# Five of the blocks that a two-layer trunk turns around: by 32x32 transposes of VectorE instead of TensorE and copies

## The chip, the cores and the metric

The kernel runs on one NeuronCore of a Trainium2 chip. The metric is the time of one execution on the device in microseconds (us), the median of several executions. The chip's engines are named as the profile names them: PE is TensorE (PEld its weight loads), DVE is VectorE, ACT is ScalarE, POOL is GpSimd, SP is SyncE, which here issues the weight transfers.

## What is computed

Two residual layers of a streaming encoder on 256 tokens of width 2048, in float32. The first layer's mixer has one input projection whose columns are q, k, v and g of a retention block and xb and gate of a gated recurrence (RG-LRU); the second layer's is windowed attention with grouped keys. Each layer ends in a squared-ReLU MLP. What matters here, cut from the reference:

```python
proj = h @ w_in                        # (256, 6144)
q, k, v, g, xb, gate = jnp.split(proj, cuts, axis=-1)
...
# RG-LRU: xc = causal 4-tap convolution of xb over time
r = sigmoid(einsum('bsnc,ncd->bsnd', xblk, w_a) + b_a)
i = sigmoid(einsum('bsnc,ncd->bsnd', xblk, w_x) + b_x)
log_a = -8 * r * softplus(-lam);  a = exp(log_a)
b = sqrt(-expm1(2 * log_a)) * i * xc
_, hh = lax.associative_scan(lru_combine, (a, b), axis=1)
lru_out = hh * gelu(gate, approximate=True)
...
q, k, v = jnp.split(h @ w_qkv, ...)    # attention: 4 key heads of 64
```

The recurrence runs along time, so xb and gate are wanted with channels on partitions and time along the free dimension; the projection gives them the other way round. The same holds for the keys of the attention.

## The kernel before

**Blocks and slots.** All dense products are cut into 89 blocks of 512 output columns (`BLOCKS`, L78): 12 of the first mixer's input projection in the order xb, gate, q, k, v, g (columns 0 to 511 of each), then the same six again, 4 of its output projection, 32 of the MLP, and so on; "kv" is the one block of keys and values of the second layer, "aq" its four query blocks. Each engine runs through the blocks in slots (`run_slots`, L182). In slot b TensorE multiplies block b in 8 halves (k = 0 to 7, 12 matmuls of 512 columns each, `products`, L1060), while ScalarE and VectorE finish block b-1 ("post", L649 and L943) at fixed halves (ticks) k of the slot, and prepare weights four halves ahead.

**Weights.** SyncE loads a block's weights in four transfers. For each half, ScalarE rounds 128x1024 values to `w_hi` (`cut_hi`, L540) and VectorE makes the rest `w_lo` (`cut_lo`, L737). At tick k of a slot both prepare half k+4, into a ring of four: `cut_hi` waits until TensorE is done with half k (`half_used`), `cut_lo` waits for `w_hi`, and TensorE's half k+4 waits for `w_lo` (`lo_ready`). Both calls stand last in a tick, behind what the tick does for the block before and for the recurrence.

**Turning a block.** ScalarE takes the finished block out of `acc` into `stage` (`leave`, L575, tick 0). For the plain kinds (xb, gate, q, k, kv, aq) TensorE then does 8 transposes of 128x128 into two PSUM banks (`turn_block`, L1097), at the end of half `TURN_AT` (2 for xb, gate and kv; 4 for q and k), and VectorE copies the two banks to the tile (L982) one tick later. The kinds "up" and "res" are turned by VectorE alone: 16 transposes of 32x256 (each four by two squares of 32x32) in `turn_quadrants` (L913), 4 at tick 1, 6 at tick 2 and 6 at tick 3 (`QUADRANTS_AT`, L98). In woven slots, of which kv's is one, everything comes two ticks later (`late`, L118).

**The recurrence.** For each of 8 channel groups n (`LRU_IN_SLOT`, L124: n = 0 in slot 2, 1 in slot 3, 4 in slot 8, 5 in slot 9) `lru` does, counted in ticks from its slot's start: convolution on VectorE at tick 2 (L820, L823); gate products on TensorE behind half 4 (L1136); sigmoids on ScalarE at tick 5 (L607) and there also the gelu's sigmoid (L610), which waits for GpSimd's polynomial of the gate (L526 to L528, `poly_done`); exp and tanh at tick 6 (L614, L616), a root at tick 7 (L620), the scan on VectorE at tick 8, that is tick 0 of the next slot (L836 to L845). GpSimd's polynomial for n = 0 and n = 4 waits for the gate block that has just been turned (`turned_out`). In slot 1, at tick 4, VectorE and ScalarE also make a small softplus table (L800 to L814; ScalarE's part is the exp of L699). In slots 3, 4, 9 and 10 VectorE rotates q or k at tick 1 (L788 to L793).

Slot by slot the blocks that the change touches are finished in slots 1 (xb, first half), 2 (gate, first half), 7 (xb, second), 8 (gate, second) and, in the second layer, that behind kv.

Of the kernel before, what the change touches and what calls it, by code (L numbers as in the profile page):

```python
# [30 lines left out]
QUADRANTS = P // QUAD  # L31
D_MODEL = 2048
SEQ = 256
TT = SEQ // P
KT = D_MODEL // P
NB = 512
# [53 lines left out]
TURNED = {"xb", "gate", "q", "k", "g", "kv", "aq", "up", "res"}  # L90
BY_QUADRANT = {"up", "res"}
SPLIT = {"g", "up", "res"}
PLAIN = TURNED - SPLIT
FROM_STAGE = {"xb", "gate", "kv", "aq"}

TURN_AT = {"aq": 0, "q": 4, "k": 4, "g": 4, "xb": 2, "gate": 2, "kv": 2}

QUADRANTS_AT = {"up": {1: 4, 2: 6, 3: 6}, "res": {1: 4, 2: 6, 3: 6}}  # L98
STATIONARY_STARTS = ({MIX_OUT0, MLP0, QKV0, ATT_OUT0, MLP1}
# [18 lines left out]
def late(b):  # L118


    return 2 if b in WOVEN else 0
# [26 lines left out]
N_EVAC_DVE = total({"res", "down", "fin"}, TT)  # L148
N_TURNED = total(TURNED, 2)
N_SPLIT = total(SPLIT, 2)  # L150

# [71 lines left out]
def build(nc, t):  # L223
    ctx = ExitStack()
    with ctx:
# [313 lines left out]
        def _(act):  # L539
# [35 lines left out]
            def leave(slot, kind, j):  # L575

                b = slot.b - 1
                act.wait_ge(half_used, slot.halves(late(b)))
                norm = NORM_OF[b]
                act.wait_ge(rinv_ready, norm + 1)  # L580
# [68 lines left out]
            def post(slot, k):  # L649
                b = slot.b - 1  # L650
                if b < 0:
                    return
                kind, j = BLOCKS[b]
                if k == late(b) and kind in BY_ACT:
                    leave(slot, kind, j)
                if k == 1 + late(b) and kind in ("res", "fin"):
                    act.wait_ge(evac_dve, slot.count(N_EVAC_DVE, 0))
                    square_sums(next_norm(b), j)
                if kind in SPLIT and k == out_at(kind, b):
                    hi, _, kt, scale = target(b)  # L660
                    for m in range(2):
                        turned_parts(hi, kt + 2 * m, None if scale is None else scale + 2 * m,
                                     slot.count(N_TURNED, -1, INIT_HALVES + m + 1), m, kind in BY_QUADRANT)
                if k == 4 and kind == "res" and j == COLS - 1:
                    root(next_norm(b))
# [62 lines left out]
        def _(dve):  # L728
# [184 lines left out]
            def turn_quadrants(slot, k, kind, j):  # L913
# [10 lines left out]
                if k == min(at) and kind == "res":  # L924
                    dve.wait_ge(evac_dve, slot.count(N_EVAC_DVE, 0))
                src = stage if kind == "up" else x[:, :, j * NB:(j + 1) * NB]
                src = src.rearrange("p t (k f c) -> p t k f c", k=COLS, f=QUADRANTS)
                dst = turn.rearrange("p m (k t a c) -> p t (m k) a c", k=2, t=TT, a=QUADRANTS)
                done = sum(n for tick, n in at.items() if tick < k)
# [4 lines left out]
                if k == max(at):  # L934
                    ins.then_inc(turned, 2)

            def plain_target(kind, j):
                if kind == "xb":
                    return lambda m: xb_t[:, 2 * m:2 * m + 2, TAPS - 1:]
                tile = {"gate": gate_t, "q": q_t, "k": k_t, "kv": kk_t, "aq": qq_t}[kind]  # L940
                return lambda m: tile[:, 2 * m:2 * m + 2, :]

            def post(slot, k):  # L943
# [30 lines left out]
                if kind in TURNED and k == out_at(kind, b):  # L974
                    for m in range(2):
# [4 lines left out]
                        elif kind in PLAIN:  # L980
                            dve.wait_ge(turned, slot.count(N_TURNED, -1, INIT_HALVES + m + 1))
                            nc.vector.tensor_copy(plain_target(kind, j)(m),  # L982
                                                  bank[:, m, :].rearrange("p (k s) -> p k s", k=2)
                                                  ).then_inc(turned_out, 1)
# [322 lines left out]
```

## Time and profile before

| what | value |
|---|---|
| median of 3 runs | 2023.03 us (2022.39 to 2023.51) |
| the profiled execution: its own time | 2022.12 us |
| its span, first to last instruction | 2020.2 us |
| PE busy | 2002.8 us (99%), 9195 matmuls |
| DVE busy | 1420.8 us (70%) |
| ACT busy | 1019.8 us (50%) |
| POOL busy | 45.2 us (2%) |
| mean granted clock of TensorE | 0.999 of full |

The share of PE is of modelled matmul ends, so "99% busy" says that it has hardly a gap, not that it is at its peak. The profile's other lists used below are: the waits (who waited for whom), the chain that ended last in order of time, and the timeline of each engine: start and length in us, the engine, the line, the operation, what is written and read, how many alike are merged into the row, and in brackets the idle time before it with what ended it.

### The profile page before, as it was taken

To read this page: it belongs to the slowest core of one execution; us is meant where nothing else is said; L and a number is where in the kernel's file an instruction comes from. 1 tells how busy PE (TensorE), PEld (TensorE's weight loads), DVE (VectorE), ACT (ScalarE), POOL (GpSimd) and SP (SyncE) were. 2 spreads that over 40 slices of the span, in tenths; PEclk is the share of its full clock that TensorE was granted. 3 is DMA by queue.
4 is the path that set the end of the run, shared out by engine and by line. 5 is a ranking of instruction groups with operands and counts; after the bars stand their busy time and mean duration, and the time that the engine had idled before them with its cause. 6 is when DMAs were issued, how large, how long until landed. Compare 5 with 4: busy or idle time off the path is not lost.

```text
span 2020.2 us, 24644 instructions
## 1 busy us (share of the span) xinstructions
PE 2002.8 (99%) x9195; PEld 1655.0 (82%) x9195; DVE 1420.8 (70%) x1932; ACT 1019.8 (50%) x1344; POOL 45.2 (2%) x55
## 2 busy tenths in 40 slices
PE   8999999999999999999999999999999999999998
PEld 6888888888888888888888877888888888888886
DVE  5776677988558657755889667988558756855875
ACT  6656665555345435434545555555435434444554
POOL 1110110000000000000000000000000000000000
PEclk9999999999999999999999999999999999999999
DMA  8556546656566565655655544566655665566563
GB/s 301 168 171 210 172 161 207 195 181 208 192 193 195 190 194 185 202 191 183 208 188 188 168 145 160 178 195 199 205 188 187 199 195 187 187 206 189 188 201 112
DMA packets 191100, 382.49 MB, mean 189 GB/s; under 512 B 6184, under 2 KB 6448, under 8 KB 190896
## 3 DMA queue, kind: packets, MB, share of 16 engines
q1 hardware_dynamic: 189776, 377.58, 57.4%
q0 software_dynamic: 1216, 3.88, 0.6%
q8 instruction: 49, 0.80, 0.2%
q14 instruction: 27, 0.22, 0.0%
q10 hardware_dynamic: 32, 0.01, 0.0%
HBM read 379.34 MB, written 2.10 MB: 189 GB/s over the span
## 4 chain that ended last, share of the span: by engine, by line
PE 95%; DVE 3%; ACT 2%; issue 0%; DMA 0%; SPq 0%; ACTq 0%
PE acc L1072 31%; PE acc L1074 30%; PE acc L1073 30%; ACT w_hi L550 1%; DVE w_lo L743 1%; PE bank L1103 1%; PE bank L1182 0%; DMA x<-in_x 0%; PE bank L1206 0%; PE bank L1192 0%; DVE area L823 0%; ACT L614 0%; ACT L620 0%; DVE turn L790 0%; PE bank L1136 0%
## 5 line engine op out<-in xcount | busy, mean ns | idle before, releaser
L743 DVE TENSOR_TENSOR w_lo<-raw,w_hi 128x1024 fp32r<-128x1024 f32 x712 | 865.3, 1224 | 538.4 <-ACT w_hi L550 535.9
L550 ACT ACTIVATE w_hi<-raw 128x1024 fp32r<-128x1024 f32 x712 | 748.1, 1059 | 811.2 <-PE acc L1074 810.2
L1072 PE MATMUL acc<-w_hi,a_hi 128*128 128x512 f32 x1568 | 615.1, 392 | 0.1
L1074 PE MATMUL acc<-w_hi,a_lo 128*128 128x512 f32 x1568 | 610.7, 389 | 0.0
L1073 PE MATMUL acc<-w_lo,a_hi 128*128 128x512 f32 x1568 | 610.5, 389 | 0.0
L1072 PE MATMUL acc<-w_hi,b_hi 128*128 128x512 f32 x1264 | 492.3, 390 | 0.0
L1073 PE MATMUL acc<-w_lo,b_hi 128*128 128x512 f32 x1264 | 491.8, 389 | 0.0
L1074 PE MATMUL acc<-w_hi,b_lo 128*128 128x512 f32 x1264 | 491.8, 389 | 0.0
L1072 PEld LDWEIGHTS acc<-w_hi,a_hi 128*128 128x128 f32 x1568 | 294.7, 188 | 62.9 <-issue 2.3
L1074 PEld LDWEIGHTS acc<-w_hi,a_lo 128*128 128x128 f32 x1568 | 294.4, 188 | 61.6
L1073 PEld LDWEIGHTS acc<-w_lo,a_hi 128*128 128x128 f32 x1568 | 294.6, 188 | 60.3
L1072 PEld LDWEIGHTS acc<-w_hi,b_hi 128*128 128x128 f32 x1264 | 237.2, 188 | 49.9 <-issue 0.7
L1074 PEld LDWEIGHTS acc<-w_hi,b_lo 128*128 128x128 f32 x1264 | 237.2, 188 | 49.2
L1073 PEld LDWEIGHTS acc<-w_lo,b_hi 128*128 128x128 f32 x1264 | 237.3, 188 | 49.2
L932 DVE STREAM_TRANSPOSE turn<-stage 32x256 f32<-32x256 f32 x512 | 223.1, 436 | 7.7
L558 ACT ACTIVATE b_hi<-turn 128x512 fp32r<-128x512 f32 x64 | 37.0, 625 | 107.1 <-DVE turn L932 107.1
L932 DVE STREAM_TRANSPOSE turn<-x 32x256 f32<-32x256 f32 x192 | 83.7, 436 | 2.9
L595 ACT ACTIVATE stage<-acc,rinv 128x512 f32<-128x512 f32 x92 | 57.6, 674 | 1.4 <-DVE rinv L776 1.4
L952 DVE TENSOR_TENSOR x<-x,acc 128x512 f32<-128x512 f32 x78 | 49.8, 679 | 0.0
L751 DVE TENSOR_TENSOR b_lo<-turn,b_hi 128x512 fp32r<-128x512 f32 x64 | 41.1, 684 | 0.0
L600 ACT ACTIVATE stage<-stage 128x512 f32<-128x512 f32 x64 | 36.7, 626 | 0.0
L560 ACT ACTIVATE a_hi<-turn,vecs 128x256 fp32r<-128x256 f32 x24 | 12.1, 502 | 35.8 <-DVE turn L932 35.8
(166 smaller groups left out, 566.6 us busy)
## 6 DMA issues: line engine op xcount, KB each, us to landing
raw<-in_mlp_w_up SPq DMA_DIRECT2D x128, 1024.0 KB, 5.5
raw<-in_mlp_w_down SPq DMA_DIRECT2D x128, 1024.0 KB, 5.1
raw<-in_hyb_w_in SPq DMA_DIRECT2D x48, 1024.0 KB, 5.2
raw<-in_attn_w_qkv SPq DMA_DIRECT2D x20, 1024.0 KB, 5.1
raw<-in_hyb_w_out SPq DMA_DIRECT2D x16, 1024.0 KB, 5.2
raw<-in_attn_w_out SPq DMA_DIRECT2D x16, 1024.0 KB, 5.2
x<-in_x SPq DMA_DIRECT2D x4, 512.0 KB, 9.7
out_y<-x SPq DMA_DIRECT2D x4, 512.0 KB, 3.0
```

The costliest lines, as they stand in the source:

```text
L550: nc.scalar.activation(w_hi[:, h % RING], raw[:, h // 2, 2 * (h % 2):2 * (h % 2) + 2, :], ACT.Copy).then_inc(hi_ready, 1)
L558: nc.scalar.activation(hi[:, kt:kt + 2, :], src, ACT.Copy).then_inc(turned_hi, 1)
L595: ins = nc.scalar.activation(stage[:, tt, :], src, ACT.Relu if kind == "up" else ACT.Copy, scale=s)
L600: nc.scalar.activation(stage[:, tt, :], stage[:, tt, :], ACT.Square).then_inc(squared, 1)
L743: nc.vector.tensor_tensor(w_lo[:, h % RING], raw[:, h // 2, 2 * (h % 2):2 * (h % 2) + 2, :], w_hi[:, h % RING].bitcast(F32), ALU.subtract) ...
L751: nc.vector.tensor_tensor(lo[:, kt:kt + 2, :], src, hi[:, kt:kt + 2, :].bitcast(F32), ALU.subtract).then_inc(turned_out, 1)
L932: ins = nc.vector.transpose(dst[f * QUAD:(f + 1) * QUAD, :, :, a, :], src[a * QUAD:(a + 1) * QUAD, :, :, f, :])
L952: nc.vector.tensor_tensor(xs, xs, acc[:, b % 2, tt, :], ALU.add).then_inc(evac_dve, 1)
L1072: nc.tensor.matmul(a, xh, wh, start=first, stop=False)
L1073: nc.tensor.matmul(a, xh, wl, start=False, stop=False)
L1074: ins = nc.tensor.matmul(a, xl, wh, start=False, stop=last)
L1103: ins = nc.tensor.transpose(bank[:, banks + m, e * SEQ + tt * P:e * SEQ + (tt + 1) * P], src[:, tt, c:c + P], ident[:, :])
```

## The change

For xb, gate and kv the 8 transposes on TensorE and the two copies on VectorE go. In their place `turn_quadrants` writes the final tile directly by 16 VectorE transposes at ticks 1, 2 and 3 (4, 6 and 6 of them). The last of the 16 gives the signal `turned_out`, which the copies gave. Since `stage` is read until then, `leave` of the block behind such a one waits for `turned_out` too. q, k and aq stay as they were.

```diff
+DIRECT = {"xb", "gate", "kv"}
+BY_QUADRANT = {"up", "res"} | DIRECT
-PLAIN = TURNED - SPLIT
-FROM_STAGE = {"xb", "gate", "kv", "aq"}
-TURN_AT = {"aq": 0, "q": 4, "k": 4, "g": 4, "xb": 2, "gate": 2, "kv": 2}
-QUADRANTS_AT = {"up": {1: 4, 2: 6, 3: 6}, "res": {1: 4, 2: 6, 3: 6}}
+PLAIN = TURNED - SPLIT - DIRECT
+FROM_STAGE = {"aq"}
+TURN_AT = {"aq": 0, "q": 4, "k": 4, "g": 4}
+QUADRANTS_AT = {kind: {1: 4, 2: 6, 3: 6} for kind in BY_QUADRANT}
...
                 act.wait_ge(half_used, slot.halves(late(b)))
+                if b > 0 and BLOCKS[b - 1][0] in DIRECT:
+                    act.wait_ge(turned_out, slot.count(N_TURNED, -1, INIT_HALVES))
...
+                if k == min(at) and kind in DIRECT:
+                    dve.wait_ge(evac_act, slot.count(N_EVAC_ACT, 0))
+                src = x[:, :, j * NB:(j + 1) * NB] if kind == "res" else stage
                 src = src.rearrange("p t (k f c) -> p t k f c", k=COLS, f=QUADRANTS)
-                dst = turn.rearrange("p m (k t a c) -> p t (m k) a c", k=2, t=TT, a=QUADRANTS)
+                if kind in DIRECT:
+                    tile = {"xb": xb_t[:, :, TAPS - 1:], "gate": gate_t, "kv": kk_t}[kind]
+                    dst = tile.rearrange("p k (t a c) -> p t k a c", t=TT, a=QUADRANTS)
+                else:
+                    dst = turn.rearrange("p m (k t a c) -> p t (m k) a c", k=2, t=TT, a=QUADRANTS)
...
                 if k == max(at):
-                    ins.then_inc(turned, 2)
+                    ins.then_inc(turned_out if kind in DIRECT else turned, 2)
```

What it moves on VectorE in slot 1, where the first xb block is finished (L743 and, in the changed kernel, L748 make `w_lo`; L800 and L805 begin the softplus). Before:

```order
L743 TENSOR_TENSOR w_lo<-raw,w_hi 128x1024 [waits hi_ready] x3
L982 COPY area<-bank 128x2x256 [waits turned] x2
L743 TENSOR_TENSOR w_lo<-raw,w_hi 128x1024 [waits hi_ready]
L800 TENSOR_SCALAR soft<-vecs 128x8 [waits vecs_ready,zeroed]
L801 TENSOR_TENSOR soft<-vecs,soft 128x8 [waits chain]
L803 TENSOR_SCALAR soft<-soft 128x8 [waits soft_exp]
```

and in the changed kernel:

```order
L748 TENSOR_TENSOR w_lo<-raw,w_hi 128x1024 [waits hi_ready]
L943 STREAM_TRANSPOSE area<-stage 32x2x4x32 [waits evac_act,turned_out]
L943 STREAM_TRANSPOSE area<-stage 32x2x4x32 x3
L748 TENSOR_TENSOR w_lo<-raw,w_hi 128x1024 [waits hi_ready]
L943 STREAM_TRANSPOSE area<-stage 32x2x4x32 x6
L748 TENSOR_TENSOR w_lo<-raw,w_hi 128x1024 [waits hi_ready]
L943 STREAM_TRANSPOSE area<-stage 32x2x4x32 x6
L748 TENSOR_TENSOR w_lo<-raw,w_hi 128x1024 [waits hi_ready]
L805 TENSOR_SCALAR soft<-vecs 128x8 [waits vecs_ready,zeroed]
L806 TENSOR_TENSOR soft<-vecs,soft 128x8 [waits chain]
L808 TENSOR_SCALAR soft<-soft 128x8 [waits soft_exp]
```

Two copies have gone and sixteen transposes stand among the four `w_lo` ahead of the softplus.

What it moves on VectorE in slot 2, where the first gate block is finished and the recurrence of n = 0 begins (the L820 and L823 rows, L825 and L828 in the changed kernel, are its convolution; "x6" and "x5" begin with the rest of slot 1). Before:

```order
L743 TENSOR_TENSOR w_lo<-raw,w_hi 128x1024 [waits hi_ready] x6
L820 TENSOR_SCALAR area<-area,vecs 128x256
L823 SCALAR_TENSOR_TENSOR area<-area,vecs 128x256 [waits chain] x3
L743 TENSOR_TENSOR w_lo<-raw,w_hi 128x1024 [waits hi_ready]
L982 COPY area<-bank 128x512 [waits turned] x2
L743 TENSOR_TENSOR w_lo<-raw,w_hi 128x1024 [waits hi_ready] x3
```

and in the changed kernel:

```order
L748 TENSOR_TENSOR w_lo<-raw,w_hi 128x1024 [waits hi_ready] x5
L943 STREAM_TRANSPOSE area<-stage 32x2x4x32 [waits evac_act,turned_out]
L943 STREAM_TRANSPOSE area<-stage 32x2x4x32 x3
L748 TENSOR_TENSOR w_lo<-raw,w_hi 128x1024 [waits hi_ready]
L943 STREAM_TRANSPOSE area<-stage 32x2x4x32 x6
L825 TENSOR_SCALAR area<-area,vecs 128x256
L828 SCALAR_TENSOR_TENSOR area<-area,vecs 128x256 [waits chain] x3
L748 TENSOR_TENSOR w_lo<-raw,w_hi 128x1024 [waits hi_ready]
L943 STREAM_TRANSPOSE area<-stage 32x2x4x32 x6
L748 TENSOR_TENSOR w_lo<-raw,w_hi 128x1024 [waits hi_ready] x3
```

Ten transposes now stand ahead of the convolution, and six behind it.

Who waits for the gate tile: ScalarE in slot 2, tick 4 to 6, the same rows in both kernels (here before; L610 is the gelu's sigmoid, which waits for GpSimd's polynomial):

```order
L550 ACTIVATE w_hi<-raw 128x1024 [waits half_used,raw_loaded0]
L607 ACT_TABLE_LOAD [waits soft_ready]
L607 ACTIVATE area<-bank,vecs 128x256 [waits gates_done]
L607 ACTIVATE area<-bank,vecs 128x256
L610 ACTIVATE area<-area 128x256 [waits poly_done]
L550 ACTIVATE w_hi<-raw 128x1024 [waits half_used]
L614 ACT_TABLE_LOAD
L614 ACTIVATE area<-area,soft 128x256 [waits sig_done]
```

Nothing moved here; the `w_hi` of the next halves and the rest of the recurrence stand behind the wait for `poly_done`.

## Rows read from the trace of the kernel before

**Rows 1.** The page, part 4: the chain that ended last, by engine.
```profile
PE 95%; DVE 3%; ACT 2%; issue 0%; DMA 0%; SPq 0%; ACTq 0%
```

**Rows 2.** The waits of the span: engine and line, releaser, us, times, longest.
```profile
PE bank L1136 <- DVE area L823: 1.2, 4, 0.3
```

**Rows 3.** The chain that ended last, in order of time: start us, us, what.
```profile
68.37 0.87 PE bank L1103 x8
```

**Rows 4.** Timeline of PE, slot 2: its first matmul, and the turn behind half 2.
```profile
60.05 0.39 PE L1072 MATMUL acc<-w_hi,a_hi 128*128 128x512 f32 x1
...
68.21 1.03 PE L1103 MATMUL bank<-ident,stage 128*128 128x128 f32 x8
```

**Rows 5.** The transposes of L932: count, duration ns min/median/max; then DVE's timeline.
```profile
L932 DVE STREAM_TRANSPOSE turn<-stage x512: 425/436/442, 425.7 to 1940.4; 32x256 f32<-32x256 f32 x171
...
401.20 2.67 DVE L932 STREAM_TRANSPOSE turn<-x 32x256 f32<-32x256 f32 x6
403.89 1.23 DVE L743 TENSOR_TENSOR w_lo<-raw,w_hi 128x1024 fp32r<-128x1024 f32 x1
```

**Rows 6.** Timeline of DVE, slot 1, from tick 0 to the weights behind the softplus.
```profile
43.88 2.36 DVE L743 TENSOR_TENSOR w_lo<-raw,w_hi 128x1024 fp32r<-128x1024 f32 x2 [2.34 <-ACT w_hi L550]
...
50.46 1.23 DVE L743 TENSOR_TENSOR w_lo<-raw,w_hi 128x1024 fp32r<-128x1024 f32 x1 [1.14 <-ACT w_hi L550]
...
56.59 3.49 DVE L743 TENSOR_TENSOR w_lo<-raw,w_hi 128x1024 fp32r<-128x1024 f32 x3
```

**Rows 7.** Timeline of ACT, slot 1: the softplus's exp begins.
```profile
52.04 1.28 ACT L699 ACT_TABLE_LOAD   x1 [1.62 <-DVE soft L801]
```

**Rows 8.** Timeline of DVE, slot 2: weights, convolution, weights, copies.
```profile
64.12 1.23 DVE L743 TENSOR_TENSOR w_lo<-raw,w_hi 128x1024 fp32r<-128x1024 f32 x1 [1.55 <-ACT w_hi L550]
...
67.92 0.41 DVE L820 TENSOR_SCALAR area<-area,vecs 128x256 f32<-128x256 f32 x1
...
69.81 1.22 DVE L743 TENSOR_TENSOR w_lo<-raw,w_hi 128x1024 fp32r<-128x1024 f32 x1
70.94 1.28 DVE L982 COPY area<-bank 128x512 f32<-128x512 f32 x2
```

**Rows 9.** Timeline of POOL: first and last operation of the polynomial, n = 0, then n = 1.
```profile
72.31 0.61 POOL L526 TENSOR_TENSOR area<-area 128x256 f32<-128x256 f32 x1 [50.60 <-DVE area L982]
...
73.50 1.59 POOL L528 TENSOR_TENSOR area<-area 128x256 f32<-128x256 f32 x1
...
89.23 1.46 POOL L526 TENSOR_TENSOR area<-area 128x256 f32<-128x256 f32 x1 [10.08 <-DVE area L845]
...
91.58 1.05 POOL L528 TENSOR_TENSOR area<-area 128x256 f32<-128x256 f32 x1
```

**Rows 10.** Timeline of ACT, slot 2: the gelu's sigmoid, and the weights behind it.
```profile
77.91 0.42 ACT L610 ACTIVATE area<-area 128x256 f32<-128x256 f32 x1
78.35 1.06 ACT L550 ACTIVATE w_hi<-raw 128x1024 fp32r<-128x1024 f32 x1
```

**Rows 11.** Timeline of DVE from slot 2's last tick on; and of PE, slot 3, gate products.
```profile
85.29 1.23 DVE L743 TENSOR_TENSOR w_lo<-raw,w_hi 128x1024 fp32r<-128x1024 f32 x1 [1.45 <-ACT w_hi L550]
...
98.53 0.70 PE L1136 MATMUL bank<-area 128*128 128x256 f32 x2 [0.30 <-DVE area L823]
```

**Rows 12.** Slot 8: DVE's weights at tick 0, and ACT's weights behind its L610.
```profile
209.26 1.23 DVE L743 TENSOR_TENSOR w_lo<-raw,w_hi 128x1024 fp32r<-128x1024 f32 x1 [1.55 <-ACT w_hi L550]
...
223.52 1.06 ACT L550 ACTIVATE w_hi<-raw 128x1024 fp32r<-128x1024 f32 x1 [1.45 <-PE acc L1074]
```

**Rows 13.** Timeline of DVE: slot 7, weights at tick 0; and the slot behind kv, tick 3.
```profile
186.61 1.23 DVE L743 TENSOR_TENSOR w_lo<-raw,w_hi 128x1024 fp32r<-128x1024 f32 x1 [1.55 <-ACT w_hi L550]
...
1122.70 0.29 DVE L971 COPY area<-area 64x256 f32<-64x256 f32 x1
```

**Rows 14.** PE's second turn of x after an idle stretch; and that stretch in windows (the 1.00 is the granted clock).
```profile
10.46 1.97 PE L1103 MATMUL bank<-ident,x 128*128 128x128 f32 x8 [2.39 <-DMA x<-in_x]
...
10.40:12.00 1.60, 1.54 (x7) 1.54 (x8) 1.60 (x4) 1.60 (x3) 0.00 (x0) 1.00 1.04 367
```

More of the change, by code:

```diff
@@ L90 @@
 TURNED = {"xb", "gate", "q", "k", "g", "kv", "aq", "up", "res"}
-BY_QUADRANT = {"up", "res"}
+DIRECT = {"xb", "gate", "kv"}
+BY_QUADRANT = {"up", "res"} | DIRECT
 SPLIT = {"g", "up", "res"}
-PLAIN = TURNED - SPLIT
-FROM_STAGE = {"xb", "gate", "kv", "aq"}
-TURN_AT = {"aq": 0, "q": 4, "k": 4, "g": 4, "xb": 2, "gate": 2, "kv": 2}
-QUADRANTS_AT = {"up": {1: 4, 2: 6, 3: 6}, "res": {1: 4, 2: 6, 3: 6}}
+PLAIN = TURNED - SPLIT - DIRECT
+FROM_STAGE = {"aq"}
+TURN_AT = {"aq": 0, "q": 4, "k": 4, "g": 4}
+QUADRANTS_AT = {kind: {1: 4, 2: 6, 3: 6} for kind in BY_QUADRANT}
 STATIONARY_STARTS = ({MIX_OUT0, MLP0, QKV0, ATT_OUT0, MLP1}
@@ L149 @@
 N_TURNED = total(TURNED, 2)
+N_MOVED = total(TURNED - DIRECT, 2)
 N_SPLIT = total(SPLIT, 2)
@@ L662, in post @@
                         turned_parts(hi, kt + 2 * m, None if scale is None else scale + 2 * m,
-                                     slot.count(N_TURNED, -1, INIT_HALVES + m + 1), m, kind in BY_QUADRANT)
+                                     slot.count(N_MOVED, -1, INIT_HALVES + m + 1), m, kind in BY_QUADRANT)
                 if k == 4 and kind == "res" and j == COLS - 1:
@@ L925, in turn_quadrants @@
                     dve.wait_ge(evac_dve, slot.count(N_EVAC_DVE, 0))
-                src = stage if kind == "up" else x[:, :, j * NB:(j + 1) * NB]
+                if k == min(at) and kind in DIRECT:
+                    dve.wait_ge(evac_act, slot.count(N_EVAC_ACT, 0))
+                src = x[:, :, j * NB:(j + 1) * NB] if kind == "res" else stage
                 src = src.rearrange("p t (k f c) -> p t k f c", k=COLS, f=QUADRANTS)
-                dst = turn.rearrange("p m (k t a c) -> p t (m k) a c", k=2, t=TT, a=QUADRANTS)
+                if kind in DIRECT:
[3 more added lines that the diff above has]
+                    dst = turn.rearrange("p m (k t a c) -> p t (m k) a c", k=2, t=TT, a=QUADRANTS)
                 done = sum(n for tick, n in at.items() if tick < k)
@@ L934, in turn_quadrants @@
                 if k == max(at):
-                    ins.then_inc(turned, 2)
+                    ins.then_inc(turned_out if kind in DIRECT else turned, 2)
             def plain_target(kind, j):
-                if kind == "xb":
-                    return lambda m: xb_t[:, 2 * m:2 * m + 2, TAPS - 1:]
-                tile = {"gate": gate_t, "q": q_t, "k": k_t, "kv": kk_t, "aq": qq_t}[kind]
+                tile = {"q": q_t, "k": k_t, "aq": qq_t}[kind]
                 return lambda m: tile[:, 2 * m:2 * m + 2, :]
@@ L980, in post @@
                         elif kind in PLAIN:
-                            dve.wait_ge(turned, slot.count(N_TURNED, -1, INIT_HALVES + m + 1))
+                            dve.wait_ge(turned, slot.count(N_MOVED, -1, INIT_HALVES + m + 1))
                             nc.vector.tensor_copy(plain_target(kind, j)(m),
```

## Prediction

> **What bounds the kernel now.** I read the chain that ended last first. It lies on PE for 95% [rows 1], so TensorE's stream of matmuls is the time, and what another engine does counts only where TensorE has to wait for it. The list of waits comes second. Behind the start, nearly the only such wait that it books to another engine is the gate product of the recurrence waiting for the convolution on VectorE: 1.2 us in four waits, the longest 0.3 [rows 2]. They stand in slots 3, 4, 9 and 10, in which VectorE rotates q or k. So these four slots have no cover left at all. Third come the timelines of VectorE, ScalarE and GpSimd in the slots that the change touches, which show how far each is ahead of TensorE there.
>
> **What goes.** A turn on TensorE adds 0.87 us to the chain [rows 3], five times: 4.35 us at most. The copies are worth 1.28 us of VectorE per block [rows 8], but only where VectorE is waited for.
>
> **What comes.** 16 transposes per block. The same form runs 704 times before at 425 to 442 ns [rows 5]; six in a row and the step to the next operation take 2.69 us (401.20 to 403.89), so four take 1.79, and a `w_lo` with the step to a transpose 1.25. A block costs VectorE 7.17 us where the copies cost 1.28. I go through the five slots and ask each time when the last work behind the transposes is ready and when it is wanted. A half on TensorE takes (68.21 - 60.05) / 3 = 2.72 us [rows 4].
>
> **Slot 1 (xb, first half).** VectorE's tick 0 starts with `w_lo` at 43.88, not changed, since that time comes from ScalarE [rows 6]. From there it never idles: 1.25 + 1.79 (four transposes) + 1.25 + 2.69 + 1.25 + 2.69 puts the `w_lo` of tick 3 at 54.80, against 50.46 before, 4.34 us later. The exp of the softplus on ScalarE starts 1.58 behind that `w_lo` (50.46 to 52.04) [rows 7], so at 56.38, and the next `w_lo` 4.55 behind the exp's start (52.04 to 56.59), so at 60.93; it ends at 62.16. That `w_lo` is of tick 4: half 0 of slot 2. TensorE, rid of one turn, wants it at 60.05 - 0.87 = 59.18 [rows 4]. So it waits 3.0 us and slot 2 starts at about 62.2 instead of 60.05. Term: **+2.2 us**. The rest of slot 1 is in time: half 7 is wanted at 62.2 - 3.0 - 2.7 = 56.5 and its `w_lo` (tick 3) ends at 56.0. Weights for halves 1 to 3 of slot 2 then follow at VectorE's pace, 1.13 us apiece, ahead of TensorE's 2.72.
>
> **Slot 2 (gate, first half).** I keep the clock of before, since all engines start this slot off TensorE. VectorE: `w_lo` at 64.12 [rows 8], then 1.25 + 1.79 + 1.25 + 2.69 = 71.10 when the ten first transposes are done. The convolution takes 1.89 (67.92 to 69.81), to 72.99. TensorE wants it behind half 4, at 68.21 + 2 x 2.72 = 73.65: just in time. Then 1.25 + 2.69: the gate tile is complete at 76.93 (before: 72.22, the end of the copies). GpSimd starts its polynomial 0.09 us behind that (72.22 to 72.31), at 77.02. The polynomial took 2.78 us for n = 0 (72.31 to 75.09), where VectorE was idle for its first part, and 3.40 for n = 1 (89.23 to 92.63) beside VectorE's work [rows 9]. VectorE now has two `w_lo` to do just there, and none behind them; I take 3.2: ready at 80.2. ScalarE's L610, which waits for it, starts at 80.25 instead of 77.91 [rows 10]: **2.35 us later**. Queued behind L610 on ScalarE are the weights `w_hi` of ticks 5, 6 and 7 and between them two table loads, exp, tanh and root, back to back in the trace; VectorE's `w_lo` of tick 7 (85.29) waits for the last of them, and from there VectorE runs without a gap (scan, `w_lo`, rotation, `w_lo`, convolution of n = 1) to TensorE's gate products at 98.53, for which TensorE already waits 0.30 [rows 11]. So the whole 2.35 arrives at TensorE in slot 3, and the turn saved in slot 2 only makes the wait longer. Term: **+2.35**. In slots 3 and 4 all then counts from TensorE again.
>
> A rule of the Trainium skill bears on this term: the page "GPSIMD Engine Reference", section "Specifications", says that GpSimd's access is shared with VectorE and contended while VectorE runs an instruction with two SBUF inputs (`w_lo` is one). The trace agrees: the same first operation took 0.61 us with VectorE idle and 1.46 beside it [rows 9]. Without such contention the polynomial would be at its 2.78 or under, and the term 1.9.
>
> **Slot 8 (gate, second half).** The same 12.81 us from the `w_lo` of tick 0 (64.12 to 76.93): 209.26 + 12.81 = 222.07 [rows 12], GpSimd 0.09 + 3.2, and 0.05 and 0.44 to the `w_hi` behind L610 (77.91 to 78.35 [rows 10]): 225.85, against 223.52. There ScalarE had 1.45 us of idle time, which is used up in this. The chain behind it is that of slot 3. Term: **+2.35** (225.85 - 223.52, rounded).
>
> **Slot 7 (xb, second half)** has no softplus and no recurrence. From 186.61 [rows 13] the `w_lo` of tick 3 is done 12.2 us later, at 198.8; TensorE wants it for half 7 at about 201.6, the turn already taken off. Cover: 2.8 us. Term: **-0.87**. **The slot behind kv**: transposes begin at 1122.99 [rows 13] and VectorE is through with them at 1132.6, level with TensorE again by the next block; the tightest `w_lo` (tick 5) ends at 1133.8 and is wanted at 1135.5. Term: **-0.87**.
>
> **The new waits.** `leave` behind a direct block waits for transposes that ended four ticks earlier: nothing.
>
> **Sum**: 2.2 + 2.35 + 2.35 - 0.87 - 0.87 = +5.2 us, on the profiled execution's own 2022.12 (its span 2020.2 and 1.9 around it). The median is 0.91 above that execution, so I add to the median: **2028.2 us**. Bounds: transposes at 425 or 442 ns move each of three terms by -0.2 or +0.1; the polynomial at 2.78 us, or half a microsecond above 3.2, moves two terms by -0.45 or +0.5; TensorE's restart in slot 2 may cost 0.2 more. That gives +3.7 to +6.7, or 2026.7 to 2029.7.
>
> **The rivals.**
> **Faster: VectorE's delay stays covered everywhere.** Then only the five turns count: -4.35, 2018.7 us. It decides where the delays shrink below their cover: in slot 1 the transposes would have to take 3.0 us less, 0.25 us apiece instead of 0.44. For it speaks that "up" and "res" blocks are turned this way without a wait on PE in the list; against it that neither has a softplus or a polynomial behind the transposes, and 704 durations that agree within 4%. The Trainium skill (page "VectorE: DVE Perf Modes", section "The three transpose paths") gives 311 ns for a 128x128 on VectorE, in bf16; a block of eight would be an estimated 2.5 us by that, and this rival would hold. The trace disagrees for float32 in this form, 7.0 us for sixteen. The same page's rules advise TensorE for a 128x128 transpose whose result may go to PSUM, which is what the kernel does before. Chance 0.08.
> **In between: L610 costs nothing.** If ScalarE's delay is caught up before slots 3 and 9 (a cover that I overlook between 78 and 98 us), those terms are 0 at best instead of 2.35, and the sum is +2.2 - 1.74 = +0.5: 2023.5. The trace speaks against it, with the waits of 0.3 at the very end of that chain [rows 2, 11]. The same result, give or take a microsecond, if the softplus is covered and L610 is not (4.7 - 3 x 0.87 = +2.1: 2025.1). Chance 0.17.
> **Dearer: TensorE restarts slowly.** It now stands for 3.0 us once and for some 2.5 us twice. After such a stretch at the start (2.39 us) eight transposes took 1.97 us instead of 1.03, at a granted clock that the windows show as 1.00 (2.4 GHz) [rows 14, 4]. Three times 0.94 more is 2031.0. The page "TensorE: Matmul & The Clock Gate" (section "The HAM clock gate") holds that an idle array is put to half its clock until it has been busy again; the row shows half speed, the windows no lower clock, so it is open. Chance 0.08.
> That the change does not do what it says I leave out: the order of instructions shows the transposes, and no turn on TensorE, in all five slots.
>
> **How the numbers follow.** The forecast's own case has 0.67. A measurement of this kernel tells about 0.2% (4 us) from no change, so slower begins at 2027.1, a microsecond below the forecast: 0.61 of the 0.67 and the dearer case, 0.69 in all. Faster begins at 2019.0: 0.07. The rest, 0.24, is within. The range holds the forecast's bounds and half of the two neighbours: 2024.5 to 2030.8.
>
> **What would show it.** Waits of PE on `w_lo` of about 3 us at the start of slot 2 (near 60 us) and on the convolution or the rotation in slots 3 and 9, 3 us or more each, with ScalarE's L610 (its new line) waiting for GpSimd for 2 to 3 us twice; transposes into `area` at 436 ns; no PE wait in slots 7 and behind kv, each 0.87 shorter. Wrong would be: no wait before slot 2 (the softplus had cover), L610 without a wait, or transposes into the tiles that cost something else than those into `turn`.

## The result, and the profile after

The changed kernel takes **2036.86 us** (median of 6 runs, 2035.6 to 2038.05), the kernel before in the same session 2022.71 us (2022.36 to 2023.51). The ratio is 1.0068, with a 95% interval of 1.0058 to 1.0078: slower by 14 us. The forecast was 2028.2 us, and 2030.8 the end of its range: the direction was right and the size too small by a factor of nearly three. The profiled execution took 2035.6 us, its span is 2033.8 (13.6 more than before).

The page of the changed kernel (TensorE's lines are 9 higher than before; L550, L610, L699, L743, L823 and L932 are now L552, L615, L704, L748, L828 and L943): one queue of part 3, the chain that ended last by engine (part 4), and one group of part 5.

```profile
q8 instruction: 66, 1.08, 0.2%
...
PE 92%; DVE 4%; ACT 2%; issue 1%; POOL 0%; DMA 0%; ACTq 0%; SPq 0%; DVEq 0%
...
L943 DVE STREAM_TRANSPOSE area<-stage 32x256 f32<-32x256 f32 x80 | 34.8, 436 | 1.2
```

PE has 92% of the chain and not 95 [rows 1]. The 80 transposes take 436 ns each, as reckoned. The first line has changed: the engines' code came in 66 packets, before in 49 (0.80 MB). I come back to it. The waits (who for whom: us in all, times, longest):

```profile
ACT area L615 <- POOL area L530: 8.7, 2, 5.1
...
ACT L704 <- DVE soft L806: 6.9, 1, 6.9
...
PE bank L1145 <- DVE area L828: 5.1, 4, 2.3
...
PE acc L1081 <- ACT stage L600: 3.0, 1, 3.0
PE bank L1112 <- DVE turn L798: 2.9, 2, 1.4
...
PE acc L1081 <- issue: 0.9, 2, 0.5
```

Of PE's four, before had only the first, with 1.2 us [rows 2]; the other three are new. ScalarE's wait on the softplus (second row) was 1.6 us before, its wait on GpSimd not there. I followed each to its place.

**Slot 1 to 2.** Timeline of the changed kernel, rows of DVE, ACT and PE in order of time:

```profile
55.07 1.23 DVE L748 TENSOR_TENSOR w_lo<-raw,w_hi 128x1024 fp32r<-128x1024 f32 x1
...
56.66 1.28 ACT L704 ACT_TABLE_LOAD   x1 [6.85 <-DVE soft L806]
...
59.20 0.39 PE L1083 MATMUL acc<-w_hi,a_lo 128*128 128x512 f32 x1
...
61.22 4.62 DVE L748 TENSOR_TENSOR w_lo<-raw,w_hi 128x1024 fp32r<-128x1024 f32 x4
...
62.58 0.77 PE L1081 MATMUL acc<-w_hi,a_hi 128*128 128x512 f32 x1 [2.99 <-ACT stage L600]
63.15 0.63 PE L1082 MATMUL acc<-w_lo,a_hi 128*128 128x512 f32 x1
63.57 0.63 PE L1083 MATMUL acc<-w_hi,a_lo 128*128 128x512 f32 x1
```

This execution is 0.33 us late from slot 1 on. Without that, the three times on VectorE and ScalarE were forecast within 0.1 (54.80, 56.38, 60.93), and slot 2's first matmul comes 2.20 late. (The list names ScalarE's copy of the finished block, which ended just then, at 62.5. It is not what TensorE waits for: before, the same copy starts at 61.21, after slot 2's first matmul at 60.05 [rows 4]. The `w_lo` of 61.22 to 62.45 is.) But then the matmuls start 0.43 us apart instead of 0.23. The windows of the changed kernel show why (us, busy and count of PE, PEld, DVE, ACT, POOL, then the granted clock):

```profile
62.00:65.00 3.00, 2.42 (x6) 1.99 (x7) 3.00 (x4) 1.10 (x2) 0.00 (x0) 0.51 0.17 20
106.00:110.00 4.00, 4.00 (x12) 3.14 (x11) 3.81 (x5) 1.15 (x3) 1.55 (x1) 0.57 0.77 247
254.00:260.00 6.00, 6.00 (x15) 4.67 (x16) 4.38 (x5) 1.14 (x3) 0.74 (x1) 0.50 0.86 297
```

TensorE ran at half clock (1.2 GHz) in three stretches, each behind one of the new waits; before, all three windows show 1.00 with 15, 20 and 28 matmuls in them.

**Slot 2 to 3.** The same timeline: POOL's polynomial, ACT behind it, and PE in slot 3:

```profile
80.92 1.65 POOL L528 TENSOR_TENSOR area<-area 128x256 f32<-128x256 f32 x1 [59.32 <-DVE area L943]
82.67 1.25 POOL L529 TENSOR_SCALAR area<-area 128x256 f32<-128x256 f32 x1
84.00 0.74 POOL L530 TENSOR_TENSOR area<-area 128x256 f32<-128x256 f32 x1
...
84.77 0.42 ACT L615 ACTIVATE area<-area 128x256 f32<-128x256 f32 x1 [3.64 <-POOL area L530]
...
101.91 1.09 PE L1112 MATMUL bank<-ident,turn 128*128 128x128 f32 x8 [1.45 <-DVE turn L798]
105.26 0.70 PE L1145 MATMUL bank<-area 128*128 128x256 f32 x2 [2.26 <-DVE area L828]
```

The polynomial took 3.82 us (80.92 to 84.74), not the 3.2 I had taken. The chain behind it is the one forecast, and it reaches TensorE twice in slot 3, at the turn of q and at the gate products. Slots 8 and 9 repeat it.

**The first MLP loop.** Timeline of PE where the loop over 8 slots of the first MLP, which runs three times, jumps back:

```profile
601.64 0.39 PE L1083 MATMUL acc<-w_hi,a_lo 128*128 128x512 f32 x1
602.39 0.49 PE L1081 MATMUL acc<-w_hi,a_hi 128*128 128x512 f32 x1 [0.36 <-issue]
...
776.36 0.39 PE L1083 MATMUL acc<-w_hi,a_lo 128*128 128x512 f32 x1
777.27 0.49 PE L1081 MATMUL acc<-w_hi,a_hi 128*128 128x512 f32 x1 [0.52 <-issue]
```

Two gaps that no engine and no transfer of data explains, in code that the change does not touch. The list of DMA queues for 590 to 900 us, which is the second and third pass, has this row in the changed kernel:

```profile
q8 instruction: 17, 0.28, 0.4%
```

In the kernel before it has no row for that queue: no code came while the loop ran again. The 17 packets are all that the changed kernel has more than before (66 against 49).

**The ledger.** Time of like events after less before, from both timelines; each line is what it grew by:

| place | forecast | measured |
|---|---|---|
| start, up to slot 1 | 0 | +0.33 |
| slot 1 to 2, wait on the softplus's chain | +2.2 | +2.20 |
| half clock behind it | 0 | +1.45 |
| slot 2 to 3, chain of the gelu's sigmoid | +2.35 | +2.75 |
| half clock behind it | 0 | +1.62 |
| slot 7, turn of xb gone | -0.87 | -0.92 |
| slot 8 to 9, the same chain | +2.35 | +2.69 |
| half clock behind it | 0 | +2.93 |
| jumps back of the first MLP loop | 0 | +0.65, +0.82 |
| kv, turn gone | -0.87 | -0.93 |
| sum | +5.2 | +13.6 |

Against the forecast that is 8.4 us more: 6.0 are the clock, 1.5 the loop, 0.7 the chain with the polynomial, 0.3 the start. My theory from here on: *the forecast's waits are right; the clock falls because of them; and the loop's gaps come from where its code lies.* The rivals: the clock falls for another reason (VectorE's load, DMA), and the loop's gaps belong to the direct transposes.

### The profile page after: what moved, and what is told of

Same layout as the page of the kernel before. It is cut to its first block, busy times and chain, and to the rows that moved or that the text cites. A ratio compares the mean times of both kernels' runs of the same rounds, so it can differ in the third digit from the quotient of the medians.

```text
span 2033.8 us, 24622 instructions
## 1 busy us (share of the span) xinstructions
PE 2005.5 (99%) x9155; PEld 1655.2 (81%) x9155; DVE 1449.9 (71%) x2002; ACT 1018.8 (50%) x1344; POOL 46.8 (2%) x55
## 4 chain that ended last, share of the span: by engine, by line
PE 92%; DVE 4%; ACT 2%; issue 1%; POOL 0%; DMA 0%; ACTq 0%; SPq 0%; DVEq 0%
PE acc L1081 30%; PE acc L1083 30%; PE acc L1082 30%; ACT w_hi L552 1%; DVE w_lo L748 1%; DVE area L943 1%; DVE area L828 0%; PE bank L1191 0%; PE bank L1215 0%; PE bank L1201 0%; PE bank L1112 0%; ACT L619 0%; ACT L625 0%; DMA x<-in_x 0%; DVE turn L795 0%
## 5 line engine op out<-in xcount | busy, mean ns | idle before, releaser
L748 DVE TENSOR_TENSOR w_lo<-raw,w_hi 128x1024 fp32r<-128x1024 f32 x712 | 865.7, 1226 | 521.3 <-ACT w_hi L552 518.4
L552 ACT ACTIVATE w_hi<-raw 128x1024 fp32r<-128x1024 f32 x712 | 747.2, 1059 | 803.0 <-PE acc L1083 802.1
L943 DVE STREAM_TRANSPOSE turn<-stage 32x256 f32<-32x256 f32 x512 | 223.0, 436 | 7.7
L943 DVE STREAM_TRANSPOSE turn<-x 32x256 f32<-32x256 f32 x192 | 83.6, 436 | 2.9
L943 DVE STREAM_TRANSPOSE area<-stage 32x256 f32<-32x256 f32 x80 | 34.8, 436 | 1.2
```

What stands on the lines that cost most here:

```text
L552: nc.scalar.activation(w_hi[:, h % RING], raw[:, h // 2, 2 * (h % 2):2 * (h % 2) + 2, :], ACT.Copy).then_inc(hi_ready, 1)
L748: nc.vector.tensor_tensor(w_lo[:, h % RING], raw[:, h // 2, 2 * (h % 2):2 * (h % 2) + 2, :], w_hi[:, h % RING].bitcast(F32), ALU.subtract) ...
L943: ins = nc.vector.transpose(dst[f * QUAD:(f + 1) * QUAD, :, :, a, :], src[a * QUAD:(a + 1) * QUAD, :, :, f, :])
```

## The experiments

Twelve kernels. In most only some of the five blocks are direct; the code for that is the change's own with a set of pairs:

```diff
-DIRECT = {"xb", "gate", "kv"}
+DIRECT = {("xb", 0)}          # or the pairs named in each experiment
```

**1 to 3: parts of the change.** xb's first half alone:

> Only the first xb block is turned by VectorE, the other four as before. Theory A (the cost is where TensorE waits, plus half clock after a long wait): one wait of 3.0 us ahead of slot 2, slot 2 starts 2.2 us later than before, its first seven matmuls at half clock add 1.4; in all +3.6 us against before, about 2026.3, with one stretch of granted clock 0.50. Theory B (every directly turned block costs alike, a fifth of the 13.6 us of the whole change): +2.7, and no such wait stands out. If the stall without the clock were all: +2.2.

Measured: 2034.54 us (2033.44 to 2036.87), ratio 1.0061 [1.0046, 1.0077]. Both gate blocks alone:

> Only the two gate blocks are turned by VectorE. Theory A: no wait ahead of slot 2; ScalarE's gelu sigmoid waits 3.6 to 5 us for GpSimd's polynomial in slots 2 and 8, TensorE reaches the gate products of n=1 and n=5 2.7 us late each, and after each wait runs at half clock for 3.4 to 6.9 us, 1.6 to 2.9 us more: +8.6 to +11.2 against before, about 2032.6. Theory B (a fifth per block): +5.4. Without the clock: +5.4 as well, but then no stretch of granted clock under 1.00 is to be seen.

Measured: 2034.82 us (2034.22 to 2035.45), ratio 1.0059 [1.0044, 1.0075]. xb's second half and kv alone, the two that I had called covered:

> Only the second xb block and kv are turned by VectorE. Theory A: both have cover, so only two turns go: -1.8 us, about 2020.9, no new wait of TensorE. Theory B (a fifth per block): +5.4. If the matmuls that are gone shift the code of TensorE's first MLP loop so that its instructions are fetched again in every pass, +1.5 on top of A, and the instruction queue shows 66 packets instead of 49.

Measured: 2029.28 us (2029.16 to 2031.33), ratio 1.0034 [1.0021, 1.0048]. The first lies 8.2 us above what theory A gave, the second 2.2, the third 8.4 (6.9 with its rider on the code), and the sum of the parts is not the whole (11.8 + 12.0 + 6.5 is over 30, the whole 14). In the third the slots behave as forecast (0.9 earlier after slot 7, no new wait on another engine above 0.3); its loss stands in the first MLP loop, +4.6 and +3.1, but for 1.2 us at the start of the profiled execution. (In these kernels the matmuls are L1085 to L1087, the gate products L1149 and the copy of the finished block L602; in some they are a few lines lower still.) Its list of waits:

```profile
PE acc L1087 <- issue: 5.5, 2, 2.8
```

And its page, part 3, the queue that brings the engines' instructions:

```profile
q8 instruction: 67, 1.10, 0.2%
```

The first kernel has the same there (5.4 in two waits, 67 packets, +3.1 and +3.2), the second two waits of 1.5 in all and 66 packets (+1.2 and +1.3). Without what the loop lost (6.3, 2.5 and 7.7 us) the three parts add up to 13.8, the whole change to 12.7. So what the loop costs does not follow the number of direct blocks. What differs is how many matmuls stand ahead of the loop: 8 fewer than before in the first and third (kv comes behind the loop), 16 fewer in the second, 32 fewer in the whole change.

**4: the whole change with the matmuls given back.** 32 tiny transposes in the idle time at the start:

```diff
             for j in range(2):
+                for _ in range(16):
+                    nc.tensor.transpose(bank[:, 2, 0:KT], vec_rows[0:KT, 0, :], ident[0:KT, 0:KT])
                 pe.wait_ge(x_loaded[j], 16)
```

> The change whole, plus 32 tiny transposes (16x16) of TensorE while it waits for x at the start, as many matmuls as the change took away ahead of the first MLP loop. Theory A (the 0.65 and 0.82 us that TensorE loses at the two jumps back in the first MLP loop are instruction fetches, which depend on where the loop's code lies): the instruction queue is back at 49 packets, both gaps are gone, and the time is 1.5 us under the whole change's (2035.4). Rival (the gaps come from VectorE's or ScalarE's lateness in the loop): 66 packets or not, the gaps stay and the time is that of the whole change, 2036.9.

Measured: 2034.31 us (2032.81 to 2036.07), ratio 1.0058 [1.0043, 1.0073]. The time is 2.5 us under the whole change's, where 1.5 was expected. The instruction queue (page, part 3) is back to what it was, none of its packets comes between 600 and 900 us, and no gap is left at the loop's jumps:

```profile
q8 instruction: 49, 0.80, 0.2%
```

What is left of the loss lies in slots 2 to 10. The next kernels keep such padding, so that the loop is out of the comparison.

**5: the two covered blocks with 8 tiny transposes.**

> The second xb block and kv turned by VectorE, as in the run before of that kind (2029.3 us), plus 8 tiny transposes of TensorE in its idle time at the start, which put the code of the first MLP loop back to where it lies in the kernel before. Theory A (code placement): the instruction queue back at 49 packets, no wait of TensorE on issue at the loop's two jumps back (5.5 us before), and the two turns that are gone are the whole effect: -1.8 us against before, about 2021.0. Rival (turning on VectorE itself slows the loop, through later weights): the time stays at 2029.

Measured: 2021.07 us (2020.26 to 2021.85, 11 runs) against 2022.85, ratio 0.9991 [0.9982, 1.0000]. Eight transposes of 16 by 16 that compute nothing turn 2029.28 into 2021.07. The forecast's two terms for covered slots (-1.74) come out as -1.8.

**6: take away what the polynomial waits for.** For n = 0 and 4, GpSimd's polynomial reads the tile of xb, which is ready long before, so the gelu of two channel groups is computed from xb and not from the gate:

```diff
-                g = gate_t[:, n % LG, :]
+                g = gate_t[:, n % LG, :] if n % LG else xb_t[:, 0, TAPS - 1:]
```

> The change whole with 32 tiny transposes at the start (that version: 2034.3 us), and GpSimd's polynomial for n=0 and n=4 reads the xb tile instead of the gate tile, so that it waits for no gate transposes (the gelu of two channel groups is computed from xb). Theory A: ScalarE no longer waits for GpSimd, TensorE reaches the gate products of n=1 and n=5 3.6 us earlier each, and the half clock behind each (1.6 us) is gone: -10.4, about 2023.9, and one stretch of granted clock 0.50, that of slot 2. Rival (VectorE's own seven microseconds of transposes are what makes slots 3 and 9 late): the waits in slots 3 and 9 stay, 2034.

Measured: 2023.46 us (2023.01 to 2024.54), ratio 1.0004 [0.9995, 1.0013]. The list of waits has no ACT on POOL any more, and PE's are these:

```profile
PE acc L1085 <- ACT stage L602: 3.4, 1, 3.4
...
PE bank L1149 <- DVE area L830: 1.2, 4, 0.3
```

The gate products are back at the 1.2 of before [rows 2], the turn of q waits for nothing, and the clock fell only behind slot 2's wait. That one dependence carries both gate terms and two of the three half-clock stretches: 10.9 us against experiment 4.

**7: move the softplus instead** into idle time of VectorE and ScalarE in slots 0 and 1:

```diff
-                    if slot.i is None and b == 1 and k == 4:
-                        softplus()
+                    if slot.i is None and b == 0 and k == 6:
+                        softplus(0)
...
+                    if slot.i is None and b == 1 and k == 0:
+                        softplus(1)
```

> The change whole with 32 tiny transposes at the start (that version: 2034.3 us), and the softplus table made earlier: its first part at tick 6 of slot 0, its rest at tick 0 of slot 1, in place of tick 4 of slot 1. Theory A: the wait of 3.0 us ahead of slot 2 shrinks to 0.3 or less and the half clock behind it (3.0 us in that run, 1.4 in the change's profile) does not come: -4.1 to -5.7, 2028.6 to 2030.2. Rival (the transposes alone are more than slot 1 covers, wherever the softplus is): the wait only shrinks to some 2 us, 2033.

Measured: 2031.17 us (2030.69 to 2032.36), ratio 1.0042 [1.0026, 1.0057]. PE's wait ahead of slot 2 is down to 0.3 and the half clock behind it is gone. The gain over experiment 4 is 3.1 and not the 4.1 to 5.7 expected. In the two profiled executions the clock fell for longer here in slots 3 and 9: nearly 7 us each at half speed, where experiment 4 has 3.4 each.

**8: keep the waits, but keep TensorE busy in them.** Extra 128x512 matmuls into an unused bank: three ahead of slot 2, one ahead of each turn of q and two behind it; the delays on VectorE, ScalarE and GpSimd stay as they are:

```diff
+            def fill(n):
+                for _ in range(n):
+                    nc.tensor.matmul(bank[:, 2, :], ident[:, :], x[:, 0, 0:NB], start=True, stop=True)
```

> The change whole, with TensorE given something to do while it waits: matmuls of 128x512 in float32 into a bank nobody reads, 3 ahead of slot 2, 1 ahead of each q turn and 2 behind it (0.85 us each), and 23 tiny transposes at the start, so that the loop's code lies as in the kernel before (comparable version without the extra matmuls: 2034.3 us). Theory A (the clock falls because TensorE stands): all waits' lengths in sum stay, but no stretch of granted clock 0.50 in slots 2, 3 and 9, which cost 6.1 us there: about 2028.2, up to 1.2 more where an extra matmul overshoots. Rival (the matmuls behind a wait are slow for another reason, weights or memory): the slow matmuls stay and the time is 2034 or more.

Measured: 2028.75 us (2027.93 to 2029.74), ratio 1.0029 [1.0018, 1.0039]. The same three windows, in this kernel:

```profile
62.00:65.00 3.00, 2.72 (x10) 1.44 (x9) 2.97 (x6) 2.18 (x4) 0.00 (x0) 1.00 0.00 0
106.00:110.00 4.00, 4.00 (x20) 3.27 (x19) 3.54 (x5) 2.31 (x5) 1.55 (x1) 1.00 0.73 241
254.00:260.00 6.00, 6.00 (x28) 4.97 (x27) 3.93 (x6) 4.37 (x6) 1.55 (x1) 1.00 0.74 214
```

ACT still waits 8.7 us for POOL and VectorE does the same work; the clock stays at 1.00, and the time is 5.6 us under experiment 4. This separates the two: the clock fell because TensorE stood, and it cost about 5.6 us. It is also nearly the forecast's own case, waits without the clock: 2028.75 beside a forecast of 2028.2, with the polynomial's 0.7 in it that the forecast lacks.

**9: a dose of the wait.** The gelu's sigmoid on ScalarE behind the `w_hi` of tick 5:

> The whole change with 32 tiny transposes at the start (as in the run of the change with the padding alone, 2034.3 us), and ScalarE's gelu sigmoid, which waits for GpSimd's polynomial, placed behind the w_hi of tick 5 instead of ahead of it. ScalarE's chain in slots 2 and 8 is then one w_hi (1.05 us) shorter behind the wait. Theory of the chain: the wait of TensorE ahead of the q turn in slots 3 and 9 shrinks from 1.45 to 0.4 us, the wait ahead of the gate products (2.26) stays, and each of the two terms is 1.05 smaller: 2032.2 us, if the clock still falls in the same places. Theory of the clock: if a shorter wait in slots 3 and 9 keeps the granted clock up there, the half-clock stretches behind them go as well, and the time is about 2029 us. Rival (nothing behind the gelu sigmoid matters): 2034.3 again.

Measured: 2036.67 us (2032.6 to 2037.3, 4 runs), ratio 1.0069 [1.0053, 1.0084]. That is neither of the two times expected (2032.2, or 2029). The `w_hi` that now ran earlier let VectorE do a third `w_lo` beside the polynomial, whose last operation slowed from 0.74 to 1.58 us (timeline of POOL, n = 0):

```profile
84.55 1.58 POOL L532 TENSOR_TENSOR area<-area 128x256 f32<-128x256 f32 x1
```

The polynomial took 4.65 us (81.48 to 86.13), which gave back 0.8 of the 1.05 gained, and the gate products still waited 2.3. What the run does show is how loose the clock's part is. In the profiled run (2032.6) no half clock is seen in slot 3 after waits of 1.33 and 2.26 us, where in the changed kernel 1.45 and 2.26 brought 3.4 us of it; the other three runs took 2036.4 to 2037.3, with a mean clock of 0.995 where the profiled one has 0.997. I put that spread down to the clock; their traces were not taken.

**10 and 11: versions that might beat both.** xb's two halves and kv direct, softplus moved, 16 tiny transposes:

> xb of both halves and kv turned directly, gate as before, softplus moved into the idle time of slots 0 and 1, 16 tiny transposes at the start so that as many matmuls stand ahead of the first MLP loop as before. Every place is then covered by my theory, and three turns of 0.87 us go: 2.6 less, 0.3 more at the start for the tiny transposes: -2.3, about 2020.5 us, no half clock and no new wait of TensorE. Rival (slot 1 has another cause of delay than the softplus): slot 2 starts late by up to 2.2 and the half clock comes back, 2023 to 2025.

Measured: 2021.20 us (2019.92 to 2021.77, 11 runs), ratio 0.9990 [0.9981, 0.9999]; no wait and no half clock of the kind above. All five direct, softplus moved, the gelu's sigmoid behind the `w_hi` of tick 7, 32 tiny transposes:

> All five blocks turned directly, with both causes of delay moved away: the softplus in the idle time of slots 0 and 1, the gelu sigmoid behind the w_hi of tick 7, and 32 tiny transposes at the start for the code's place. If the waits on the softplus and on the polynomial are all that the change adds, five turns go (-4.35) and the tiny transposes cost 0.3 at the start: about 2018.8 to 2019.5 us, no half clock, TensorE's waits in slots 3, 4, 9 and 10 at 0.3 each. Rival (VectorE's ten transposes ahead of the convolution, or those beside the scan, add a wait of their own): one or two stretches of half clock stay, 2022 to 2026.

Measured: 2020.27 us (2019.67 to 2021.37, 11 runs) against 2022.97, ratio **0.9987 [0.9978, 0.9996]**, mean clock 0.999. Both are faster than either kernel, if only by 0.1%. The second lies 0.8 above its expectation, and one wait accounts for that (the gate products, in its list of waits):

```profile
PE bank L1157 <- DVE area L837: 2.4, 4, 0.6
```

That is 1.2 us more than the 0.3 four times that I expected. It does not come from the ten transposes ahead of the convolution: the whole change with the padding (experiment 4) has them too, and waits 0.30 and 0.27 us in slots 4 and 10, where this kernel waits 0.60. It comes from the moved sigmoid. GpSimd's last product of the gelu waits for it and now runs beside a product of VectorE ahead of the scan (n = 0, timelines of DVE and POOL):

```profile
86.37 0.72 DVE L854 TENSOR_TENSOR area<-area 128x256 f32<-128x256 f32 x1
...
85.97 0.85 POOL L534 TENSOR_TENSOR area<-area 128x256 f32<-128x256 f32 x1 [4.60 <-ACT area L618]
```

All seven such products profiled here take 0.72 us, where those of the kernel before (L840) take 0.42: 0.3 us more on the chain that ends at the gate products, in each of the four slots.

**12: the kernel before, with nothing of the change,** and 120 tiny transposes at the start:

> The kernel before, with nothing of the change, and 120 tiny transposes on TensorE in the idle time at the start. Theory of the code's place: how often TensorE's instructions of the first MLP loop are fetched again depends only on how many matmuls stand ahead of it; 120 more leave it where 8 fewer would (if the place counts modulo 128 matmuls), and that is the case of xb1 and kv alone without padding: 67 packets on the instruction queue, two stops of 2.7 to 3.2 us at the loop's jumps back, and 5 to 6 us more in the loop. The start costs 1 to 3 us more. Rival (the stops belong to the direct transposes and the padding only shifted something else): no stop at the jumps back, 49 packets, the time of before plus the start. If only absolute size counts and not the place modulo 128, the number of packets will be neither 49 nor 67.

Measured: 2040.28 us (2038.3 to 2041.15), ratio 1.0082 [1.0067, 1.0098]. Its list of waits:

```profile
PE acc L1073 <- issue: 6.2, 2, 3.4
```

And part 3 of its page:

```profile
q8 instruction: 68, 1.11, 0.2%
```

The two stops at the loop's jumps back are there, 3.4 and 2.8 us, in a kernel without one direct transpose, and 14 packets of code come between 600 and 900 us; with the half clock behind the stops the loop loses 6.2 and 4.6. The rival is out. The count is 68 and not 67; the code of 120 more matmuls is itself about one packet (0.80 MB / 49 is 16 KB; that the 68th is this one I only infer). The start cost 8.1 us where I expected 1 to 3: 120 transposes do not fit into its idle time.

## Why the prediction was wrong

**The waits: right, place by place.** These came as forecast: the softplus's chain in slot 1 (+2.2, measured +2.20), the transposes at 436 ns, the chain from the polynomial through L610 and the `w_hi` behind it to slots 3 and 9, the covered slots 7 and behind kv (-0.87, measured -0.92 and -0.93). Experiments 5 to 8 each moved one of them and the time followed. Both "faster" and "in between" fail: the softplus's wait came in full, and experiment 6 shows that the sigmoid's wait is what arrives in slots 3 and 9.

**The step that failed: "TensorE restarts slowly", chance 0.08, three times 0.94 us.** The mechanism was on the list, as a rival; the sum gave it nothing, and the bounds 0.2 us in slot 2, a figure that no run shows. I had weighed an idle stretch of 2.39 us at the start [rows 14], where the windows print 1.00, and called the half clock open. That 1.00 was no reading. In the trace of before the record of the granted clock begins only at 13.8 us, and a window ahead of that prints 1.00 all the same. The matmuls say what the clock was (timeline of PE, before; last a window over the first of them):

```profile
12.52 0.77 PE L1072 MATMUL acc<-w_hi,a_hi 128*128 128x512 f32 x1
13.08 0.63 PE L1073 MATMUL acc<-w_lo,a_hi 128*128 128x512 f32 x1
13.51 0.54 PE L1074 MATMUL acc<-w_hi,a_lo 128*128 128x512 f32 x1
13.89 0.40 PE L1072 MATMUL acc<-w_hi,a_hi 128*128 128x512 f32 x1
14.12 0.40 PE L1073 MATMUL acc<-w_lo,a_hi 128*128 128x512 f32 x1
...
12.40:13.80 1.40, 1.31 (x4) 1.12 (x4) 1.40 (x2) 1.17 (x5) 0.00 (x0) 1.00 1.05 386
```

The second and third are 0.43 us apart, like those of the half-clock stretch in slot 2; from 13.9 us on they are 0.23 apart. The first turn of x took 1.97 us like the second. So TensorE ran at half clock from its first turn on, and the row could speak neither for nor against a fall in mid-stream.

In the changed kernel the windows do show the fall, 0.50 behind a wait of 3.0 us in slot 2 and behind waits of 1.4 and 2.3 with a turn between them in slots 3 and 9. It cost 1.45, 1.62 and 2.93, together 6.0, and experiment 8 removes it with the delays in place. Even the rival's price, 2.8 us for three falls, was too small by half. The Trainium skill (page "TensorE: Matmul & The Clock Gate", section "The HAM clock gate") says that an array that has been idle is put to 1.2 GHz until it has been busy for a while, and that how many matmuls are slow at a kernel's start varies from run to run. I set one row against this rule, and the row did not bear on it. The traces agree with it, also in that the slow stretch varies (3.4 us behind slot 2's wait here, nearly 7 in experiment 4). How long a stop it takes stays open: in experiment 9 waits of 1.33 and 2.26 us brought a fall in slot 9 and none in slot 3.

**A step that was missing: where the loop's code lies.** +1.5 in the change, +7.7 in experiment 3, +10.8 in experiment 12. "What goes" counted the 40 matmuls that the change takes away as time and never as code. The runs show that the number of matmuls ahead of the first MLP loop decides: as before (experiments 4 to 11) 49 packets and no gap; 8, 16 and 32 fewer, 66 or 67 packets and gaps at both jumps back; 120 more, 68 packets and gaps too. The Trainium skill (page "Runtime: NRT & Kernel Launch", section "Instruction fetch mechanics") gives TensorE an instruction memory of 128 KiB filled in blocks of 16 KiB, or 256 instructions, and says that a taken branch to a target outside the current two blocks has to fetch it first. My estimate from these figures: 128 matmuls with their weight loads fill a block, and a loop of 768 of them fills six. By the rule of the two blocks such a loop would stop at every jump in every kernel. The traces differ there: with 49 packets no code comes in the second and third pass, and nothing stops, so the loop's code is still held. Why other places lose it is my guess: it depends on where the loop begins within a block. By that guess 120 more is like 8 fewer, which experiment 12 was built on. It agrees, but it doesn't show the rule of 128, since every number of matmuls ahead other than before's own that was run brought the gaps. Why 8 fewer costs more than 32 fewer is not settled either.

**A term mis-sized: the polynomial**, 3.82 us and not 3.2. I took a value between an idle VectorE (2.78) and the n = 1 case (3.40) and had the row's other end in the bounds only as "half a microsecond above". In the changed kernel two `w_lo` run beside it, in experiment 9 three, and it took 3.82 and 4.65. Of these 0.6 us, 0.40 and 0.34 show in the two gate terms (+2.75 and +2.69 for +2.35); where the rest went is not traced.

**The range.** Its bounds varied the sizes of terms in the sum. The two things that broke it were not in the sum at all. With them gone the forecast misses by about 1 us, inside the range.

## What to carry to other kernels

When a change makes TensorE stand in the middle of a dense stream, price the wait and the half clock behind it together: here three delays that cost 7.6 us brought 6.0 us of slow clock. If the wait can't be removed, a few matmuls into a bank that nobody reads hold the clock. And if a change adds or removes TensorE instructions ahead of a hardware loop, look at the instruction queue's packets in the profile before blaming the change: a few instructions of padding may be worth more than the edit.

## What I had not expected of the hardware

- Whether the code of TensorE's loop of 768 matmuls comes again in each pass (17 packets, or none) turns on 8 matmuls far ahead of it. The stops at a jump were 0.4 to 3.4 us, and one of about 3 us can bring half clock behind it: in experiment 12 both did, and the loop lost 10.8 us with stops of 6.2; in experiment 1 two stops of 2.7 brought none.
- The same waits gave stretches of half clock of different length in different kernels (none, some 3 or some 7 us), and the runs of one kernel that has them spread over up to 5 us, where those of a kernel without them stay within 2.
- TensorE starts at half clock, and when it rises differs by execution: the matmuls came to their 0.23 us at 13.9 us in the profiled execution of before and at 16.5 in that of experiment 3, which began slot 1 later by 1.2 us. The windows do not show it.
- A polynomial of three GpSimd operations took 2.78, 3.40, 3.82 and 4.65 us, by how much of VectorE's `w_lo` ran beside it; a single operation went from 0.74 to 1.58. VectorE pays too: 0.72 us for 0.42 beside a GpSimd product.
